# Issuing a third of the expert weights' transfers from the Activation queue in a two-layer MoE encoder

## The chip, the cores and the metric

The kernel runs on one core of a Trainium2 chip. The metric is the device time of one execution in microseconds (us). The engines are named PE (TensorE, matmuls), PEld (its weight loads), DVE (VectorE), ACT (ScalarE), POOL (GpSimd) and SP (SyncE, which here issues transfers and computes nothing). A name with a q (SPq) means the engine's instruction queue: what it issues or waits for itself. Transfers are done by 16 DMA engines that all issuing engines share.

## The reference, cut to what matters

An encoder trunk of two layers over 256 tokens of 1024 numbers, all float32. Layer 0 mixes tokens with causal pooling, layer 1 with differential attention. Each layer then has a mixture of experts: 32 experts, each token goes to two of them.

```python
for i in range(DEPTH):                       # 2 layers
    h = rms_norm(x, norm_mix_g[i])
    x = x + (pool_mixer(...) if i % 2 == 0 else diff_attention(...))
    h = rms_norm(x, norm_ffn_g[i])
    x = x + hier_moe(h, ...)
return rms_norm(x, final_g)

# in hier_moe, for the tokens xb of each expert e:
a = jax.nn.silu(xb @ w1[e]) * (xb @ w3[e])   # w1, w3: 1024 x 512
y = a @ w2[e]                                # w2: 512 x 1024
```

Each of w1, w3 and w2 has 2 MB per expert, so the experts' weights are 6 MB each and 403 million bytes in all; each weight is used once.

## The kernel before

**Order.** The five engines each run an instruction stream written out by hand, and wait for each other by semaphores. The pooling mixer, the router, the experts of layer 0, attention, the router and the experts of layer 1 follow each other. The router's numbers (`cnt`, a place for each token) are ready before the expert loop starts (`s_route`).

**The ring.** Expert weights come into `ring`, eight slots (`RING = 8`) of 2 MB each. An expert takes three chunks (`CPE = 3`): chunk 0 has the first half of w1 and of w3 (along the contracted dimension), chunk 1 the second half of both, chunk 2 all of w2. Each chunk is two transfers of 1 MB, which add to one semaphore, `loaded[slot]`. Chunk number c of a layer (c = 3e + j for chunk j of expert e) lies in slot c % 8. All 192 chunks of the two layers, and attention's eight chunks between them, are issued by SP, in exactly this order of numbers. SP issues the first eight of layer 0 at the start; those of layer 1 as attention's own chunks are used up (`attn_used`). Every later chunk c waits (L279) until chunk c - 8 is used: that is the semaphore `half` where c - 8 is a chunk 0 (PE has done the products with the first half), `gu` where it is a chunk 1 (the gate and up products are done), `y` where it is a chunk 2 (the down product is done). So w2 of expert e + 2 follows `half` of expert e; the first half of w1 and w3 of expert e + 3 follows `gu` of expert e; their second half follows `y` of expert e. In layer 0, attention's chunks follow behind the last expert's on the same queue.

**The expert loop.** Each of PE, DVE, ACT and SP runs four iterations (`ITERS = 4`) of eight experts (`BODY = 8`), in groups of four experts (`E4 = 4`). For one expert PE does the gate and up products (`gate_up`, L427, two halves of 32 matmuls; up to 32 tokens; a second block if there are more), gathers tokens of the next group (`gather`, L394), waits for the activated product, transposes it (L447), and does the down product (`down`, L465). After four experts the results are added to the tokens (`scatter`, L480). Between `gu` and the transpose stand: on ACT the Exp (L730), then on DVE one plus, reciprocal and two products (L1022 to L1028). ACT then copies the gathered tokens (L720), at the second expert of a group also the gates (L734), and after the down product its half of the result (L738); DVE copies the transposed product (L1051) and the other half (L1054). `keep_clock` issues matmuls whose results nobody reads (L346).

**The stages around it.** After the last expert of a layer follow the scatter, the residual sum on DVE (L1088), the norm, and in layer 0 the transposes (L338) and attention's products (L586 for v, L600 for q and k, L654 for the output); in layer 1 the final norm and the store of the result. POOL loads two rows of gains during attention (L327, L329), repeated over 128 partitions.

**The fallback.** If an expert had more than 64 tokens, more passes would follow, for which SP loads all chunks again (L291 to L301). In this case's data it does not run.

Of the kernel before, what the change touches and what calls it, by code (L numbers as in the profile page):

```python
# [35 lines left out]
E4 = P // SB  # L36
GPB = 2
BODY = GPB * E4
ITERS = NE // BODY
# [54 lines left out]
def build(nc, x, norm_mix_g, norm_ffn_g, pool_w, pool_scale, wq, wk, wv, wo, lq1, lk1, lq2, lk2, subln_g,  # L94
          moe_wg, moe_bg, moe_we, moe_be, moe_w1, moe_w3, moe_w2, final_g, consts, out):
    with ExitStack() as ctx:
# [122 lines left out]
        def chunk_parts(layer, e, j):  # L219

            if j < 2:
                return [(m * 2048, w[layer, e, :, :].rearrange("(p k) n -> p k n", k=KT)[:, 4 * j:4 * j + 4, :])
                        for m, w in ((0, moe_w1), (1, moe_w3))]
            w = moe_w2[layer, e, :, :].rearrange("(j p) n -> p j n", p=P)
            return [(m * 2048, w[:, 2 * m:2 * m + 2, :]) for m in range(2)]
# [17 lines left out]
        def _(sp):  # L243
# [25 lines left out]
            for layer in range(2):  # L269
                for c in range(RING):  # L270
                    if layer == 1:
                        sp.wait_ge(*attn_used[c])
                    load(c, chunk_parts(layer, c // CPE, c % CPE), loaded[c])
                steady = CPE * BODY

                def stream(it, c):

                    e, j = divmod(c - RING, CPE)
                    sp.wait_ge(used[j], it * BODY + (layer * NE + e + 1))  # L279
                    load(c % RING, chunk_parts(layer, it * BODY + c // CPE, c % CPE), loaded[c % RING])  # L280

                with sp.Fori(0, ITERS - 1) as it:
                    for c in range(RING, RING + steady):
                        stream(it, c)
                for c in range(RING, steady):
                    stream(ITERS - 1, c)

                fb = more[layer]
                sp.wait_ge(s_route, layer + 1)
                most = sp.value_load(cnt[0:1, NE + NGRP:NE + NGRP + 1], min_val=0, max_val=S)  # L290
                with sp.If(most > CAP):  # L291

                    sp.wait_ge(main["y"], NE * (layer + 1))
                    with sp.Fori(0, PASSES - 1) as m:
                        with sp.If(most > CAP * m + CAP):
                            with sp.Fori(0, NE) as e:
                                n = m * NE + e
                                for j in range(CPE):
                                    load(j, chunk_parts(layer, e, j), fb[f"wl{j}"])
                                sp.wait_ge(fb["y"], n + 1)  # L300
                                sp.sem_inc(fb["passed"], 1)  # L301
                if layer == 0:
                    for c in range(ACH):
                        e, j = divmod(CPE * NE - RING + c, CPE)
                        sp.wait_ge(used[j], e + 1)
                        load(c, attn_parts(c), loaded[c])
# [386 lines left out]
        def _(act_e):  # L693
# [29 lines left out]
                for r in range(E4):  # L723
                    gathered(s, 0, r, rounds + r + 1)

            def group(s, g, u, rounds):
                for k in range(E4):
                    n1 = g * E4 + (k + 1)
                    act_e.wait_ge(s["gu"], n1)
                    act_e.activation(sg[:, 0, :, :], gu_ps[:, :, 0, :], ACT.Exp, scale=-1.0).then_inc(s["exp"], 1)  # L730
                    gathered(s, 1 - u, k, rounds + k + 1)
                    if k == 1:
                        act_e.wait_ge(s["gt"], g + 1)
                        act_e.copy(gateT[:, :, :], gt_ps).then_inc(s["gtc"], 1)  # L734

                    act_e.wait_ge(s["y"], n1)
                    for i in (2, 3):
                        ins = act_e.copy(y[SB * k:SB * (k + 1), :, 256 * i:256 * (i + 1)],  # L738
                                         y_ps[SB * i:SB * (i + 1), :, :])
                    ins.then_inc(s["yc_a"], 1)  # L740

            def experts(layer):
                act_e.wait_ge(s_route, layer + 1)
                first_gathered(main, layer * (NGRP + 1) * E4)
                with act_e.Fori(0, ITERS) as it:
                    for gg in range(GPB):
                        group(main, it * GPB + (layer * NGRP + gg), gg % 2,
                              it * (GPB * E4) + (layer * (NGRP + 1) + gg + 1) * E4)
                fb = more[layer]
                most = act_e.value_load(cnt[0:1, NE + NGRP:NE + NGRP + 1], min_val=0, max_val=S)  # L750
                with act_e.If(most > CAP):
                    with act_e.Fori(0, PASSES - 1) as m:
                        with act_e.If(most > CAP * m + CAP):
                            first_gathered(fb, m * ((NGRP + 1) * E4))
                            with act_e.Fori(0, NGRP // 2) as pair:
                                for u in range(2):
                                    group(fb, m * NGRP + pair * 2 + u, u, (m * (NGRP + 1) + pair * 2 + (u + 1)) * E4)

            def route(layer):

# [458 lines left out]
```

## Time and profile before

| | us |
|---|---|
| median of three runs | 1174.48 |
| lowest and highest | 1172.45, 1177.19 |
| the profiled execution | 1172.21 |
| its span (first to last instruction) | 1170.4 |
| PE busy | 888.4 |
| DVE busy | 352.2 |
| ACT busy | 216.5 |
| transfers | 427.70 MB, 365 GB/s over the span |

The profile is of one execution. Each time in it is from the start of its span. A row of a view names the line of the kernel, the engine, the operation, and what it writes and reads; `x` is a count. An idle time in brackets stands before the instruction that ended it, with what released it; "issue" is idle time that no semaphore explains. The row of an issued transfer is the time that the issuing engine spends on it; the landing is reported separately. The clock named PEclk is the share of full speed that PE was granted.

### The profile page before, as it was taken

The numbers are of one execution on the slowest core, as the hardware profiler recorded it, in microseconds if no ns is written. First come the engines' busy times: TensorE is split into PE (matmuls) and PEld (weight loads), VectorE is DVE, ScalarE is ACT, GpSimd is POOL, SyncE is SP. The second block draws the span as 40 slices with busy tenths as digits, with TensorE's granted clock in tenths as the row PEclk, the third lists the DMA queues.
The fourth block names the chain that finished last, engine by engine and source line by source line (L and its number), as shares of the span: only waits on it lengthen the run. The fifth ranks groups of instructions, "written<-read, shape, count | busy, mean of one in ns | idle before, by whom it ended". The sixth has DMA issues, their size and how long they took to land.

```text
span 1170.4 us, 20054 instructions
## 1 busy us (share of the span) xinstructions
PE 888.4 (76%) x8020; PEld 496.3 (42%) x8021; DVE 352.2 (30%) x814; ACT 216.5 (18%) x487; POOL 5.1 (0%) x15
## 2 busy tenths in 40 slices
PE   6878777766776677678999987898776757677765
PEld 4544434332433343333787554454433423334332
DVE  3523322221331222223156433222322312222223
ACT  3221212110111111111145312111111111112111
POOL 1000000000000000000000000000000000000000
PEclk9899979988998889899999989999998999888898
DMA  9979999999999999998503439999999999999992
GB/s 307 399 311 414 415 415 416 416 416 415 416 416 416 415 415 416 416 416 353 199 1 147 173 141 418 415 416 416 415 415 415 415 416 416 417 414 416 416 413 114
DMA packets 78121, 427.70 MB, mean 365 GB/s; under 512 B 7492, under 2 KB 8772, under 8 KB 43672
## 3 DMA queue, kind: packets, MB, share of 16 engines
q1 hardware_dynamic: 77528, 424.20, 88.8%
q8 instruction: 131, 2.15, 0.7%
q0 software_dynamic: 448, 1.25, 0.5%
q14 instruction: 14, 0.11, 0.0%
HBM read 424.37 MB, written 1.05 MB: 363 GB/s over the span
## 4 chain that ended last, share of the span: by engine, by line
SPq 41%; PE 30%; DMA 19%; DVE 5%; issue 4%; ACT 2%; DVEq 0%; ACTq 0%
SPq L247 40%; DMA ring<-in_moe_w 18%; PE ps L427 7%; PE ps L600 5%; PE ps L465 3%; PE ps L586 2%; PE ps L394 2%; PE ps L480 2%; PE ps L654 2%; DVE work L1024 1%; PE ps L379 1%; PE ps L346 1%; PE ps L561 1%; PE ps L374 1%; PE ps L338 1%
## 5 line engine op out<-in xcount | busy, mean ns | idle before, releaser
L427 PE MATMUL ps<-ring,work 128*32 128x256 f32 x4224 | 304.6, 437 | 178.7 <-DMA ring<-in_moe_w 123.9
L427 PEld LDWEIGHTS ps<-ring,work 128*32 128x32 f32 x4224 | 144.3, 123 | 331.3 <-DMA ring<-in_moe_w 151.2
L394 PE MATMUL ps<-work,h_sb 128*128 128x256 f32 x576 | 153.5, 412 | 7.1 <-ACT work L720 4.5
L1022 DVE TENSOR_SCALAR work<-work 128x128 f32<-128x128 f32 (+1 forms) x64 | 14.7, 230 | 476.5 <-ACT work L730 476.5
L465 PE MATMUL ps<-ring,work 128*32 128x256 f32 x2112 | 129.3, 386 | 25.7 <-DVE work L1051 25.5
L394 PEld LDWEIGHTS ps<-work,h_sb 128*128 128x128 f32 x576 | 110.2, 202 | 59.0 <-issue 38.6
L1054 DVE COPY hT<-ps 32x512 f32<-32x512 f32 x128 | 87.4, 683 | 139.5 <-PE ps L465 138.6
L730 ACT ACTIVATE work<-ps 128x256 f32<-128x256 f32 x64 | 24.6, 384 | 485.3 <-PE ps L427 485.3
L738 ACT COPY hT<-ps 32x512 f32<-32x512 f32 x128 | 74.1, 579 | 169.0 <-PE ps L465 168.3
L465 PEld LDWEIGHTS ps<-ring,work 128*32 128x32 f32 x2112 | 63.4, 110 | 75.6 <-DVE work L1051 32.7
L480 PE MATMUL ps<-hT,work 128*128 128x512 f32 x136 | 62.6, 604 | 11.1 <-DVE hT L1054 11.1
L720 ACT COPY work<-ps 128x512 f32<-128x512 f32 x72 | 42.2, 586 | 132.1 <-PE ps L394 126.7
L1024 DVE RECIPROCAL work<-work 128x128 f32<-128x128 f32 (+1 forms) x64 | 62.6, 978 | 2.2
L600 PE MATMUL ps<-hT,ring 128*128 128x256 f32 x256 | 56.5, 379 | 0.0
L600 PEld LDWEIGHTS ps<-hT,ring 128*128 128x128 f32 x256 | 48.2, 190 | 7.1 <-issue 0.5
L346 PE MATMUL ps<-cst,small 128*128 128x512 f32 x78 | 43.5, 645 | 3.5 <-issue 3.5
L480 PEld LDWEIGHTS ps<-hT,work 128*128 128x128 f32 x136 | 24.5, 189 | 49.2 <-issue 49.2
L447 PE MATMUL ps<-cst,work 128*128 128x128 f32 x64 | 20.7, 323 | 29.1 <-DVE work L1028 28.7
L1051 DVE COPY work<-ps 128x256 f32<-128x256 f32 x64 | 27.2, 425 | 50.0 <-PE ps L447 50.0
L447 PEld LDWEIGHTS ps<-cst,work 128*128 128x128 f32 x64 | 9.1, 142 | 56.7 <-issue 56.6
L654 PE MATMUL ps<-ring,work 128*128 128x512 f32 x64 | 28.6, 594 | 0.0
L586 PE MATMUL ps<-ring,hT 128*128 128x512 f32 x64 | 27.9, 594 | 0.8 <-DVE hT L918 0.8
(151 smaller groups left out, 454.9 us busy)
## 6 DMA issues: line engine op xcount, KB each, us to landing
ring<-in_moe_w SPq DMA_DIRECT2D x384, 1024.0 KB, 21.8
ring<-in_attn_wv SPq DMA_DIRECT2D x4, 1024.0 KB, 18.5
ring<-in_attn_wq SPq DMA_DIRECT2D x4, 1024.0 KB, 20.3
ring<-in_attn_wk SPq DMA_DIRECT2D x4, 1024.0 KB, 22.7
ring<-in_attn_wo SPq DMA_DIRECT2D x4, 1024.0 KB, 21.5
x_sb<-in_x SPq DMA_DIRECT2D x2, 512.0 KB, 6.3
work<-in_pool_w SPq DMA_DIRECT2D x1, 1024.0 KB, 12.9
out_x<-h_sb SPq DMA_DIRECT2D x2, 512.0 KB, 2.7
```

Of the source, the lines that this page charges most:

```text
L247: sp.dma_start(ring[:, slot, at:at + k * n].rearrange("p (k n) -> p k n", k=k), src) \
L346: pe.matmul(ps[:, bank, :], zero, cst[:, 0:512], start=True, stop=True)
L394: mm = pe.matmul(xg_ps[:, q, :], h_sb[:, t, kt * P:(kt + 1) * P], onehot[:, u, t].rearrange("p b e s -> p (b e s)"), start=(t == 0), stop= ...
L427: mm = pe.matmul(gu_ps[SB * j:SB * (j + 1), b, :, :], xg[:, u, 4 * half + q, b, k, :], w[:, :, q, P * j:P * (j + 1)], start=(half == 0 and ...
L465: mm = pe.matmul(y_ps[SB * i:SB * (i + 1), b, :], actT[:, b, SB * j:SB * (j + 1)], w[:, j, 256 * i:256 * (i + 1)], start=(j == 0 and b == ...
L480: mm = pe.matmul(acc[:, t, i, :], gateT[:, b, t * P:(t + 1) * P], y[:, b, 512 * i:512 * (i + 1)], start=False, stop=False, skip_group_chec ...
L586: mm = pe.matmul(ps[:, 2 * t + i, :], hT[:, kt, t * P:(t + 1) * P], matrix(0, kt)[:, 512 * i:512 * (i + 1)], start=(kt == 0), stop=(kt == ...
L600: mm = pe.matmul(ps[:, h % 2, i * S:(i + 1) * S], matrix(2 + 2 * i, kt)[:, h * P:(h + 1) * P], hT[:, kt, :], start=(kt == 0), stop=(kt == ...
L654: mm = pe.matmul(ps[:, 2 * t + i, :], qT[:, h, t * P:(t + 1) * P], matrix(6, h)[:, 512 * i:512 * (i + 1)], start=(h == 0), stop=(h == NH - 1))
L738: ins = act_e.copy(y[SB * k:SB * (k + 1), :, 256 * i:256 * (i + 1)], y_ps[SB * i:SB * (i + 1), :, :])
L1024: ve.reciprocal(sg[:, 2, b, :], sg[:, 1, b, :]).then_inc(s["sig"], 1)
L1054: ins = ve.tensor_copy(y[SB * k:SB * (k + 1), :, 256 * i:256 * (i + 1)], y_ps[SB * i:SB * (i + 1), :, :])
```

## The change

The transfers of chunk 2 (w2) of experts 2 to 31 of each layer leave SP's stream and are issued by ACT, into ACT's own hardware queue. SP issues in the loop only chunks 0 and 1, under the same waits as before. ACT issues w2 of expert e + 2 in expert e, directly behind its wait for `gu` of expert e and ahead of the Exp. Since `gu` comes after `half` of the same expert, no wait of its own is added for the slot. The first eight chunks of a layer, which include w2 of experts 0 and 1, are still SP's, as are attention's chunks and the fallback. So that nothing is issued beyond expert 31, ACT's loop runs three iterations, and the fourth is written out behind it.

```diff
                 with sp.Fori(0, ITERS - 1) as it:
                     for c in range(RING, RING + steady):
-                        stream(it, c)
+                        if c % CPE < 2:
+                            stream(it, c)
                 for c in range(RING, steady):
-                    stream(ITERS - 1, c)
+                    if c % CPE < 2:
+                        stream(ITERS - 1, c)
...
-            def group(s, g, u, rounds):
+            def down_weights(layer, it, k):
+
+                c = CPE * (k + 2) + 2
+                for at, src in chunk_parts(layer, it * BODY + (k + 2), 2):
+                    n, m = view(src)
+                    act_e.dma_start(ring[:, c % RING, at:at + n * m].rearrange("p (k n) -> p k n", k=n), src) \
+                        .then_inc(loaded[c % RING], 16)
+
+            def group(s, g, u, rounds, load):
                 for k in range(E4):
                     n1 = g * E4 + (k + 1)
                     act_e.wait_ge(s["gu"], n1)
+                    load(k)
                     act_e.activation(sg[:, 0, :, :], gu_ps[:, :, 0, :], ACT.Exp, scale=-1.0).then_inc(s["exp"], 1)
...
-                with act_e.Fori(0, ITERS) as it:
+                def body(it, last):
                     for gg in range(GPB):
+                        def load(k, gg=gg):
+                            if not last or gg * E4 + k + 2 < BODY:
+                                down_weights(layer, it, gg * E4 + k)
+
                         group(main, it * GPB + (layer * NGRP + gg), gg % 2,
-                              it * (GPB * E4) + (layer * (NGRP + 1) + gg + 1) * E4)
+                              it * (GPB * E4) + (layer * (NGRP + 1) + gg + 1) * E4, load)
+
+                with act_e.Fori(0, ITERS - 1) as it:
+                    body(it, False)
+                body(ITERS - 1, True)
```

## Rows read from the trace of the kernel before

**Rows 1.** The page: span, and GB/s of all transfers in 40 equal slices.
```profile
span 1170.4 us, 20054 instructions
...
GB/s 307 399 311 414 415 415 416 416 416 415 416 416 416 415 415 416 416 416 353 199 1 147 173 141 418 415 416 416 415 415 415 415 416 416 417 414 416 416 413 114
```

**Rows 2.** Stretches (us): each engine's busy time, PEclk, DMA share, GB/s.
```profile
200.00:280.00 80.00, 57.30 (x581) 29.24 (x582) 21.97 (x45) 12.37 (x23) 0.00 (x0) 0.91 1.02 416
...
570.00:578.00 8.00, 8.00 (x38) 7.03 (x38) 0.00 (x0) 0.65 (x2) 0.00 (x0) 1.00 1.01 405
...
1143.00:1156.00 13.00, 8.10 (x78) 4.16 (x72) 2.18 (x5) 0.97 (x2) 0.00 (x0) 0.87 0.34 139
```

**Rows 3.** Groups by line: count, busy us, mean ns, idle us before with its releasers.
```profile
L427 PE MATMUL ps<-ring,work 128*32 128x256 f32 x4224 | 304.6, 437 | 178.7 <-DMA ring<-in_moe_w 123.9 <-issue 53.3 <-ACT work L720 1.5
...
L427 PEld LDWEIGHTS ps<-ring,work 128*32 128x32 f32 x4224 | 144.3, 123 | 331.3 <-DMA ring<-in_moe_w 151.2 <-issue 121.4
...
L465 PEld LDWEIGHTS ps<-ring,work 128*32 128x32 f32 x2112 | 63.4, 110 | 75.6 <-DVE work L1051 32.7 <-issue 7.7 <-DMA ring<-in_moe_w 1.7
```

**Rows 4.** The page: the chain that ended last, by engine, share of span.
```profile
SPq 41%; PE 30%; DMA 19%; DVE 5%; issue 4%; ACT 2%; DVEq 0%; ACTq 0%
```

**Rows 5.** L247 from 200 to 480 us: issue in ns (min/median/max), landing after it.
```profile
L247 SPq DMA_DIRECT2D ring<-in_moe_w x110: 383/2144/5955, 198.4 to 478.4; - x110
...
DMA to landing us min/median/max: 14.6/22.1/24.7
```

**Rows 6.** SP in order of time at both restarts: start, us, instructions merged.
```profile
64.31 0.99 SPq L247 DMA_DIRECT2D ring<-in_moe_w  x2
...
66.03 0.34 SPq L247 DMA_DIRECT2D ring<-in_moe_w  x1
...
698.47 0.97 SPq L247 DMA_DIRECT2D ring<-in_moe_w  x2
...
700.67 0.35 SPq L247 DMA_DIRECT2D ring<-in_moe_w  x1
...
706.07 0.81 SPq L247 DMA_DIRECT2D ring<-in_moe_w  x2
```

**Rows 7.** The last w2 issue of each layer (line L247): start, landing after it.
```profile
L247 SPq DMA_DIRECT2D ring<-in_moe_w x1: 2292/2292/2292, 497.0 to 497.0; - x1
...
DMA to landing us min/median/max: 22.7/22.7/22.7
...
L247 SPq DMA_DIRECT2D ring<-in_moe_w x1: 2287/2287/2287, 1129.8 to 1129.8; - x1
...
DMA to landing us min/median/max: 23.8/23.8/23.8
```

**Rows 8.** PE in order of time behind the last chunks of both layers.
```profile
514.60 1.93 PE L427 MATMUL ps<-ring,work 128*32 128x256 f32 x32 [3.09 <-DMA ring<-in_moe_w]
...
536.83 10.57 PE L586 MATMUL ps<-ring,hT 128*128 128x512 f32 x24 [0.78 <-DVE hT L918]
...
1148.68 3.35 PE L427 MATMUL ps<-ring,work 128*32 128x256 f32 x32 [4.38 <-DMA ring<-in_moe_w]
...
1155.54 1.93 PE L465 MATMUL ps<-ring,work 128*32 128x256 f32 x32 [0.52 <-DVE work L1051]
```

**Rows 9.** ACT's Exp in order of time: experts 0, 8, 16; 0, 2, 29.
```profile
65.88 0.38 ACT L730 ACTIVATE work<-ps 128x256 f32<-128x256 f32 x1 [3.87 <-PE ps L427]
...
172.23 0.38 ACT L730 ACTIVATE work<-ps 128x256 f32<-128x256 f32 x1 [17.22 <-PE ps L427]
...
295.13 0.38 ACT L730 ACTIVATE work<-ps 128x256 f32<-128x256 f32 x1 [17.06 <-PE ps L427]
...
700.51 0.38 ACT L730 ACTIVATE work<-ps 128x256 f32<-128x256 f32 x1 [4.36 <-PE ps L427]
...
720.08 0.39 ACT L730 ACTIVATE work<-ps 128x256 f32<-128x256 f32 x1 [4.03 <-PE ps L427]
...
1120.89 0.38 ACT L730 ACTIVATE work<-ps 128x256 f32<-128x256 f32 x1 [9.00 <-PE ps L427]
```

More of the change, by code:

```diff
@@ L756, in experts @@
                                 for u in range(2):
-                                    group(fb, m * NGRP + pair * 2 + u, u, (m * (NGRP + 1) + pair * 2 + (u + 1)) * E4)
+                                    group(fb, m * NGRP + pair * 2 + u, u, (m * (NGRP + 1) + pair * 2 + (u + 1)) * E4, lambda k: None)
             def route(layer):
```

## The prediction, made before the change was built

> **What bounds the kernel now.** Read the slices first: outside the start, the attention stage and the end, the transfers run at 413 to 418 GB/s [rows 1]. In a stretch of the loop the DMA share is 1.02 and the rate 416 [rows 2]. TensorE's largest wait there is for the ring at L427, the gate and up products: 123.9 us, and 151.2 us on its weight loads; at L465, the down product, the weight loads wait 1.7 us for a DMA [rows 3]. So w2 is there in time already; what comes too late is w1 and w3, and above all the second half of them. I name the chunks of expert k a(k), b(k) (its two halves of w1 and w3) and w2(k), k from 0 to 31 in a layer; each is two transfers of 1 MB.
>
> The chain puts 41% on SP's queue, L247 [rows 4], and in the loop a transfer's issue takes SP 2.14 us in the median and up to 5.96 [rows 5]. That looks like an issue bound and isn't one: with few transfers outstanding a pair of issues takes 0.97 to 0.99 us and the first alone 0.34 or 0.35 of a next pair [rows 6], so the rest of the 2.14 us is SP held back by a full queue. Transfers land 14.6 to 24.7 us after issue in the loop [rows 5]; at 2.5 us for 1 MB (416 GB/s) that is up to some nine outstanding. The kernel is bound by the rate of the transfers, and SP's queue is served in the order in which TensorE needs the chunks.
>
> From this follows a layer's length. The transfers stop once the ring's 8 chunks are full and start again when the first chunk is freed: at 64.31 and 698.47 us [rows 6]. From there they never stop until w2(31) has landed: issued at 497.0, landed 22.7 later, 519.7; and 1129.8 + 23.8 = 1153.6 [rows 7]. That is 455.4 and 455.1 us. The last chunk that TensorE waits for is b(31): its products start at 514.60 and 1148.68, after waits of 3.09 and 4.38 us for the DMA, while the last down product starts at 1155.54 behind DVE, not behind w2 [rows 8]. b(31) lands one chunk, 5 us, ahead of w2(31), and all that follows hangs on it.
>
> **The change part by part.**
>
> *Moved issues.* 30 chunks a layer, w2(2) to w2(31): 120 of the 384 transfers go from SP to ACT; the first 8 chunks of a layer stay with SP, as does the fallback. Bytes and slots are the same, so at the same rate a layer's stretch from restart to last landing stays 455.4 and 455.1 us. SP gives up issues that were waits for room: nothing gained.
>
> *The wait.* w2(k+2) took the slot of a(k) and was issued after a(k)'s products (`half`); now ACT issues it after b(k)'s (`gu`). In the loop that is no delay: SP issued the second half of the last w2 at 1129.8, and ACT sees the `gu` of two experts back at 1120.89, 9 us before [rows 7, 9]. At the restart it is one: there `half` of expert 0 starts the engines, and the next chunk, a(3), comes with `gu` at 66.03 and 700.67, so **+1.7 and +2.2 us** [rows 6]. They don't run dry again behind it: two chunks start together, 10 us of work, and b(3) was issued 5.4 us after a(3) (706.07 in layer 1, [rows 6]).
>
> *The order at the end.* With two queues w2(31) no longer stands behind b(31). When TensorE has done b(29), ACT issues w2(31); still to come are a(30), b(30), a(31), b(31) and w2(31), 25 us. If the engines share half and half, w2(31) is through after 10 us, at one third after 15, both before b(31) at 25. So b(31) lands last, where w2(31) did: at 66.03 + 455.4 = 521.4 against 514.6 (**+6.8**, of which 5.1 is the order and 1.7 the restart). The chain behind it up to the attention matmuls is TensorE, DVE and ACT, and attention's own chunks aren't in it: v's products start at 536.83 behind DVE [rows 8], while their two chunks follow w2(31) at 5 us each, some 530. Layer 1 restarts at 700.67 + 6.8 = 707.5; plus 455.1 is 1162.6 against 1148.68, **+13.9 us** in all. What follows b(31) to the end, 21.7 us, stays.
>
> *ACT's time.* Each expert gets two issues ahead of the Exp. Between 0.97 us for a pair (SP with an empty queue, [rows 6]) and 4.3 (twice its median in the loop, [rows 5]), longer if held as SP was at worst. Behind the Exp are four DVE steps, the transpose and the down product; behind it on ACT also the gather's copy, which TensorE's next gather needs. I take 1.0, since ACT's own queue holds two to four transfers, not nine. What hides it: experts 0 to 7 of layer 0, which mostly find their chunks loaded, take 172.23 - 65.88 = 106.4 us, the next eight 122.9, so TensorE has 16.5 us over in eight experts, 2.1 each [rows 9]. At 4.3 that cover is gone; the rival below prices it. The last two experts issue nothing.
>
> *Loop peeled on ACT, more code in it.* TensorE's own loop turns stand in these times, and no slice of the loops falls under 413 GB/s for them [rows 1]; a turn on ACT lies under the same cover. Zero; up to 1 us a turn is hidden too.
>
> *Two queues on the same engines.* The nearest row is the stretch in which POOL's loads of gains (L327, L329) run beside SP's: share 1.01, 405 GB/s, against 1.02 and 416 for one queue [rows 2]. So from nothing to 2.7% of 910 us, +24.6 us. POOL's loads repeat one row 128 times, which ACT's don't, so I take zero.
>
> The Trainium skill ("DMA: Bandwidth & Descriptors", section "Queues, rings and completion order") says that each DMA engine goes round robin over the queues with work, packet by packet; by it w2(31) passes b(31) as assumed, and no run before this one shows it. If instead the order of issue held, the sum would be 1178.4.
>
> **Sum.** 1.7 + 5.1 + 2.2 + 4.9 = 13.9. The profiled execution took 1172.2 us with a span of 1170.4; the median of three is 1174.5; the span stands in [rows 1]. Span 1184.3, median 1174.5 + 13.9 = **1188.4 us**, +1.2%.
>
> **The rivals.**
> - *ACT is held at its issues* (slower still). If SP's blocked issue keeps ACT waiting, a pair costs 4.3 us or more ahead of the Exp, over the 2.1 of cover. For it: SP is in L247 nearly without a break in the loop. Against: it corrects itself, since a later TensorE frees slots later, SP's queue empties and issues are short again; the engines stay busy. It costs where no backlog is left, at the end: from b(29)'s products to b(31)'s there are 25 us, and two experts take 19.6 at TensorE's best (700.51 to 720.08, [rows 9]), so 5.4 are over; of a delay of 4.3 on each of the two issues before them, and of products at the lower clock (3.35 us for a half instead of 1.93, [rows 8]), about 4 a layer comes out: 1196.5. A chance of 0.12. The Trainium skill ("Perfetto Trace Analysis", section "DMA Instruction — HWDGE (DVE, Sync)") says that the descriptor generator is locked by one sequencer until its descriptors are made; it would be the mechanism of this rival.
> - *Two queues cost rate*: 405 instead of 416 gives 1188.4 + 24.6 = 1213. It decides from 0.3% of rate, 3 us. A chance of 0.10.
> - *w2 stays last* (no change). If ACT's queue is served behind SP's backlog, b(31) lands as before and only the restarts remain: 1174.5 + 3.9 = 1178.4, within 0.5%. For it: SP's backlog is large. Against: w2 would then have to get less than a fifth of the engines over 25 us, and the down products, starved all along, would show it. Here too belongs a partial gain at the ragged end: from 1143 to 1156 us the share is 0.34, some DMA engines being done long before the last [rows 2]; if two queues took half of that out, 4 to 5 us a layer, the sum is about 1179. A chance of 0.15 for both.
> - *SP's issuing is the bound* (faster). For it: 41% of the chain. A third of its issues gone, up to 120 x 2.14 = 257 us; TensorE's waits at L427 cap it at 123.9, so down to 1050, and any tenth of that, 12 us, makes it 1162 with nothing lost. The Trainium skill ("Perfetto Trace Analysis", section "DMA Optimizations") advises to spread transfers over issuing engines where the issuing engine's track is solid; here it is. Against: issues of 0.35 us on an empty queue, and a rate that never leaves 416. With other gains of rate from two queues 0.11.
> - *The code doesn't do what it says*: 120 issues would be missing on ACT's queue; the diff leaves no way for that. 0.01, at the old time.
>
> **How the numbers follow.** The forecast has 0.51, with its own range of 1184 to 1194 (TensorE at the lower clock behind b(31), 1.5 us a layer, and up to 2 us a layer if its last two experts don't keep up). Over the rivals the range is 1175 to 1213: it leaves out the faster case and what lies above 1213, under 2 in 10. A run of this kernel can tell about 0.5%, 5.9 us. Slower by more: 0.51 + 0.12 + 0.10 = 0.73; within: 0.16; faster: 0.11.
>
> **What would show it.** Right: 120 L247-like issues on ACT's queue, a pair near 1 us; SP's median issue well under 2 us; the engines' restart at `gu`; the last landing being w1 or w3 of expert 31, TensorE's longest wait before b(31), then 21 to 22 us to the end; rate 414 to 417 still. TensorE's waits at L427 grow by some 5 us a layer plus what now isn't waited elsewhere. Wrong: a rate under 412 or above 420 in the loops; Exp starting over 2 us behind `gu` as a rule; the down products waiting for the ring; w2(31) landing after b(31).

## The result, and the profile after

The changed kernel takes 1189.72 us (median of four runs, 1188.56 to 1191.48) beside 1174.57 us for the kernel before, executed alongside it: a ratio of 1.0129, with a 95% interval of 1.0104 to 1.0155, or 15.2 us. Forecast were 13.9 us. The profiled execution took 1188.56 us with a span of 1186.8, which is 16.4 more than [rows 1].

First the page of the kernel after: span, slices of GB/s, the chain by engine, and the transfers of each issuing engine (count, KB each, median us to landing).

```profile
span 1186.8 us, 20061 instructions
...
GB/s 308 389 293 415 415 414 416 415 416 415 415 416 415 416 416 414 416 418 297 177 1 141 176 113 408 415 415 416 413 415 415 416 414 416 416 416 415 416 393 86
...
PE 50%; DMA 25%; DVE 10%; issue 7%; ACTq 4%; ACT 2%; DVEq 0%; SPq 0%
...
ring<-in_moe_w SPq DMA_DIRECT2D x264, 1024.0 KB, 24.0
ring<-in_moe_w ACTq DMA_DIRECT2D x120, 1024.0 KB, 22.6
```

Set beside [rows 1, 4]: 120 transfers have moved, the loops still run at 413 to 418 GB/s (408 in the slice that holds the restart of layer 1), and SP's 41% of the chain has become nothing. A third of the issues went to another engine, the engine that stood for 41% of the chain isn't on it any more, and the kernel is slower. The two loops as one stretch each (columns as in [rows 2]) say the same, 416 and 415 against 416:

```profile
200.00:280.00 80.00, 56.15 (x618) 30.19 (x611) 20.73 (x42) 12.65 (x24) 0.00 (x0) 0.91 1.02 416
...
750.00:1100.00 350.00, 258.12 (x2776) 137.49 (x2776) 94.16 (x188) 53.39 (x100) 0.00 (x0) 0.93 1.02 415
```

So nothing is lost in the loops. What is lost lies at their two ends. The timeline of the kernel after has both ends of both layers: start and duration in us, what, and in brackets the idle time before it.

```profile
66.40 0.83 SPq L247 DMA_DIRECT2D ring<-in_moe_w  x2
66.40 1.03 ACTq L734 DMA_DIRECT2D ring<-in_moe_w  x2
67.47 0.38 ACT L742 ACTIVATE work<-ps 128x256 f32<-128x256 f32 x1 [5.09 <-issue]
...
517.77 1.91 PE L430 MATMUL ps<-ring,work 128*32 128x256 f32 x32
522.61 1.93 PE L430 MATMUL ps<-ring,work 128*32 128x256 f32 x32 [2.93 <-DMA ring<-in_moe_w]
...
538.93 5.49 PE L349 MATMUL ps<-cst,small 128*128 128x512 f32 x6 [3.51 <-issue]
...
710.72 1.00 ACTq L734 DMA_DIRECT2D ring<-in_moe_w  x2
...
1164.91 2.94 PE L430 MATMUL ps<-ring,work 128*32 128x256 f32 x32 [3.25 <-DMA ring<-in_moe_w]
...
1171.89 1.93 PE L468 MATMUL ps<-ring,work 128*32 128x256 f32 x32 [0.52 <-DVE work L1071]
```

At 66.40 us SP issues a(3) and ACT issues w2(2) in the same moment; in [rows 6] the engines were started 1.7 us ahead of that by `half`. And where b(31)'s products started at 514.60 and 1148.68 us [rows 8], they start at 522.61 and 1164.91.

The last issues of each queue in layer 1 (issue in ns, time of issue, and then us to landing), first SP's b(31), then ACT's second half of w2(31):

```profile
L247 SPq DMA_DIRECT2D ring<-in_moe_w x1: 433/433/433, 1131.6 to 1131.6; - x1
...
DMA to landing us min/median/max: 33.2/33.2/33.2
...
L734 ACTq DMA_DIRECT2D ring<-in_moe_w x1: 488/488/488, 1140.2 to 1140.2; - x1
...
DMA to landing us min/median/max: 22.3/22.3/22.3
```

b(31) is issued 8.6 us ahead of w2(31) and lands 2.3 us behind it: 1131.6 + 33.2 = 1164.8 against 1140.2 + 22.3 = 1162.5. TensorE starts on it 0.1 us later. In [rows 7] it was w2(31) that landed last, at 1153.6, 4.9 us behind the start of b(31)'s products. In layer 0 it is the same: b(31) at 522.6 (490.2 + 32.4), w2(31) at 519.7 (494.4 + 25.3).

The lead of w2(31) is small because it isn't alone in ACT's queue: w2(30), whose second half was issued at 1125.4 us, lands only at 1147.6, 7.8 us after w2(31) was issued, and w2(31) follows 14.9 us behind it. Its row:

```profile
L734 ACTq DMA_DIRECT2D ring<-in_moe_w x1: 378/378/378, 1125.4 to 1125.4; - x1
...
DMA to landing us min/median/max: 22.2/22.2/22.2
```

**Where the 16.4 us of the span are**, each stretch before and after:

| stretch | before | after | more |
|---|---|---|---|
| start to first restart | 64.31 | 66.40 | 2.1 |
| restart to b(31)'s products, layer 0 | 450.3 | 456.2 | 5.9 |
| from there to SP's first expert chunk of layer 1 (before 565.47, after 574.80) | 50.9 | 52.2 | 1.3 |
| from there to the second restart (698.47, 710.72) | 133.0 | 135.9 | 2.9 |
| restart to b(31)'s products, layer 1 | 450.2 | 454.2 | 4.0 |
| from there to the end | 21.7 | 21.9 | 0.2 |

Of the 2.1, 1.7 are the step from `half` to `gu`; the other 0.4 had come up before it. Of the 2.9, 2.2 are that step. The stretch from restart to last landing was 455.4 and 455.1 us before; after, it is 456.2 and 454.1.

The groups of TensorE in the loop and of the instruction that waits for it, after (L430, L468, L450 are the L427, L465, L447 of before):

```profile
L430 PE MATMUL ps<-ring,work 128*32 128x256 f32 x4224 | 280.1, 410 | 113.3 <-DMA ring<-in_moe_w 63.0 <-issue 48.6 <-ACT work L723 1.5
...
L468 PE MATMUL ps<-ring,work 128*32 128x256 f32 x2112 | 164.2, 465 | 28.9 <-DVE work L1071 24.4 <-DMA ring<-in_moe_w 4.1
...
L450 PE MATMUL ps<-cst,work 128*128 128x128 f32 x64 | 21.2, 332 | 101.3 <-DVE work L1048 100.8 <-issue 0.4
```

And two of these groups in the kernel before:

```profile
L465 PE MATMUL ps<-ring,work 128*32 128x256 f32 x2112 | 129.3, 386 | 25.7 <-DVE work L1051 25.5
...
L447 PE MATMUL ps<-cst,work 128*128 128x128 f32 x64 | 20.7, 323 | 29.1 <-DVE work L1028 28.7 <-issue 0.2
```

TensorE waits 60.9 us less for the ring at the gate and up products (123.9 in [rows 3], now 63.0) and 72.1 us more at the transpose (28.7, now 100.8), behind ACT's issues: 1.2 us for each of the 60 experts that issue. This looks like a 72 us loss and a 61 us gain. It is neither, it is the same slack in another place; a4_behind_exp, below, moves it back. Along with the idle time went the lower clock: the down products behind it take 34.9 us more busy time (129.3, now 164.2) and the gate and up products 24.5 less (304.6, now 280.1).

### The profile page after: what moved, and what is told of

Same layout as the page of the kernel before. It is cut to its first block, busy times and chain, and to the rows that moved or that the text cites. A ratio compares the mean times of both kernels' runs of the same rounds, so it can differ in the third digit from the quotient of the medians.

```text
span 1186.8 us, 20061 instructions
## 1 busy us (share of the span) xinstructions
PE 895.0 (75%) x8020; PEld 503.4 (42%) x8021; DVE 352.0 (30%) x814; ACT 215.7 (18%) x487; POOL 5.1 (0%) x15
## 4 chain that ended last, share of the span: by engine, by line
PE 50%; DMA 25%; DVE 10%; issue 7%; ACTq 4%; ACT 2%; DVEq 0%; SPq 0%
DMA ring<-in_moe_w 24%; PE ps L430 15%; PE ps L468 10%; PE ps L483 5%; PE ps L603 5%; ACTq L734 4%; DVE work L1044 3%; PE ps L397 2%; PE ps L589 2%; PE ps L657 2%; DVE work L1071 1%; PE ps L349 1%; ACT work L742 1%; PE ps L450 1%; DVE work L1048 1%
## 5 line engine op out<-in xcount | busy, mean ns | idle before, releaser
L430 PE MATMUL ps<-ring,work 128*32 128x256 f32 x4224 | 280.1, 410 | 113.3 <-DMA ring<-in_moe_w 63.0
L430 PEld LDWEIGHTS ps<-ring,work 128*32 128x32 f32 x4224 | 142.4, 118 | 248.4 <-issue 105.0
L468 PE MATMUL ps<-ring,work 128*32 128x256 f32 x2112 | 164.2, 465 | 28.9 <-DVE work L1071 24.4
L397 PE MATMUL ps<-work,h_sb 128*128 128x256 f32 x576 | 149.0, 402 | 6.4 <-ACT work L723 4.5
L397 PEld LDWEIGHTS ps<-work,h_sb 128*128 128x128 f32 x576 | 107.1, 196 | 53.7 <-issue 34.6
L468 PEld LDWEIGHTS ps<-ring,work 128*32 128x32 f32 x2112 | 73.8, 129 | 95.0 <-issue 40.9
L450 PE MATMUL ps<-cst,work 128*128 128x128 f32 x64 | 21.2, 332 | 101.3 <-DVE work L1048 100.8
L450 PEld LDWEIGHTS ps<-cst,work 128*128 128x128 f32 x64 | 9.0, 140 | 131.7 <-issue 131.7
## 6 DMA issues: line engine op xcount, KB each, us to landing
ring<-in_moe_w ACTq DMA_DIRECT2D x120, 1024.0 KB, 22.6
```

What stands on the lines that cost most here:

```text
L397: mm = pe.matmul(xg_ps[:, q, :], h_sb[:, t, kt * P:(kt + 1) * P], onehot[:, u, t].rearrange("p b e s -> p (b e s)"), start=(t == 0), stop= ...
L430: mm = pe.matmul(gu_ps[SB * j:SB * (j + 1), b, :, :], xg[:, u, 4 * half + q, b, k, :], w[:, :, q, P * j:P * (j + 1)], start=(half == 0 and ...
L468: mm = pe.matmul(y_ps[SB * i:SB * (i + 1), b, :], actT[:, b, SB * j:SB * (j + 1)], w[:, j, 256 * i:256 * (i + 1)], start=(j == 0 and b == ...
```

## The experiments

My theory, from the prediction: the kernel is bound by the rate of the transfers, and the loss is made of two things that have nothing to do with who issues. The order of the last two landings is swapped (b(31) last instead of w2(31)), and the engines restart at `gu` instead of `half`. Its rivals: what is lost comes from ACT's time at its issues, or from two queues sharing the engines.

**Each part alone, on SP's one queue.** These three start from the kernel before, and ACT issues nothing in them. b1_order swaps the last two chunks of each layer:

```diff
-                for c in range(RING, steady):
+                for c in (*range(RING, steady - 2), steady - 1, steady - 2):
                     stream(ITERS - 1, c)
```

> The kernel before with one queue as it was; only the last two chunks of each layer change places in SP's stream, so that w2 of expert 31 goes ahead of the second half of w1 and w3 of expert 31. My theory (the order of the last landings is worth 5.1 and 4.9 us, and no second queue is needed for it): +10.0 us over the kernel before, 1184.5. Rival 'two queues or ACT's hold make the loss': 1174.5, since neither is in this kernel.

Measured: 1186.53 us beside 1173.08, a ratio of 1.0119 (1.0099 to 1.0140): 13.5 us by the medians, 14.0 by the ratio; 10.0 had been expected, and the interval (11.6 to 16.4 us) leaves that out. TensorE's timeline at both ends of b1_order:

```profile
520.34 3.64 PE L427 MATMUL ps<-ring,work 128*32 128x256 f32 x32 [8.20 <-DMA ring<-in_moe_w]
...
528.15 1.93 PE L465 MATMUL ps<-ring,work 128*32 128x256 f32 x32 [0.52 <-DVE work L1051]
...
1162.07 3.64 PE L427 MATMUL ps<-ring,work 128*32 128x256 f32 x32 [9.17 <-DMA ring<-in_moe_w]
...
1169.87 1.93 PE L465 MATMUL ps<-ring,work 128*32 128x256 f32 x32 [0.52 <-DVE work L1051]
```

and the clock over the first of these groups of products (columns as in [rows 2]):

```profile
520.30:524.00 3.70, 3.67 (x33) 1.48 (x33) 0.00 (x0) 0.00 (x0) 0.00 (x0) 0.50 1.01 423
```

Behind 8.2 us of idle time TensorE has a granted clock of 0.50, its 1.2 GHz level, and the 32 matmuls take 3.64 us instead of 1.93; behind the 9.17 of layer 1 they take 3.64 too. From the start of b(31)'s products to the down product there are 7.81 and 7.80 us; in the kernel before 5.43 and 6.86 (514.60 to 520.03, and 1148.68 to 1155.54 [rows 8]). That is 2.4 + 0.9 = 3.3 us on top of the 10.0 of the order: 13.3. In the trace the order itself is 5.1 and 4.9 us, as forecast: from the restarts (64.90 and 706.92) to b(31)'s products there are 455.4 and 455.2 us, against 450.3 and 450.2.

In layer 0 of the changed kernel this doesn't occur, although b(31) lands just as late. There the transfers of w2 share the engines with those ahead of b(31) and hold them back: a(31) lands at 516.5 us (issued at 481.15, landed 35.3 later), its products start at 517.77, and b(31)'s wait is only 2.93 us. Over b(31)'s products the clock is 1.00:

```profile
522.60:524.50 1.90, 1.89 (x33) 0.97 (x33) 0.00 (x0) 0.00 (x0) 0.00 (x0) 1.00 1.00 414
```

In layer 1 b(31)'s products take 2.94 us behind 3.25 of waiting, at a clock of 0.64; from their start to the down product there are 6.98 us, nearly the 6.86 of the kernel before. A short wait alone doesn't settle the clock: behind 3.0 to 3.1 us the same 32 matmuls took 1.93 us in layer 0 of the kernel before and of b2_wait_gu, but 3.44 in a1_half and 3.53 and 3.62 in b4_hold5.

b2_wait_gu lets SP wait for `gu` where it waited for `half`:

```diff
-                    sp.wait_ge(used[j], it * BODY + (layer * NE + e + 1))
+                    sp.wait_ge(used[max(j, 1)], it * BODY + (layer * NE + e + 1))
```

> The kernel before with one queue in the same order; only w2 of experts 2 to 31 waits for the gate and up products of two experts back (gu) instead of the first half of them (half). My theory: only the restart of the transfers in each layer moves, +1.7 and +2.2, so +3.9 us, 1178.4. Rival 'a later wait costs all along the loop': up to 1.9 us for each of 60 experts, over 1200. Rival 'the restart is hidden': 1174.5.

Measured: 1177.49 us beside 1173.08, 1.0035 (1.0021 to 1.0049), 4.1 to 4.4 us: as expected. Its SP queue at the restarts, to be set against [rows 6]:

```profile
66.84 0.99 SPq L247 DMA_DIRECT2D ring<-in_moe_w  x2
...
705.36 0.97 SPq L247 DMA_DIRECT2D ring<-in_moe_w  x2
```

The first restart is 2.5 us later than there (1.7 for the step to `gu`, and 0.8 that stand ahead of it), the second 6.9 us in all.

b3_order_wait has both edits.

> Both of the last two in one kernel, still with one queue and nothing on ACT. My theory: they add up to the whole loss less what the second queue and ACT's issues cost: 1174.5 + 13.9 = 1188.4 against 1189.7 for the changed kernel. Rival 'the second queue or ACT's hold makes a large part': clearly under 1185.

Measured: 1189.47 us beside 1173.08, 1.0137 (1.0113 to 1.0161), 16.1 to 16.4 us. The interval holds the changed kernel's 1.0129. A kernel with one queue, nothing issued by ACT and nothing new in its instruction stream is as slow as the changed one, once it has its order and its wait. As to size, the 3.3 us of clock are in this run and not in the changed kernel, so the two agree less closely than their times make it seem (b(31)'s products take 3.47 and 3.64 us in it, behind 8.18 and 7.97 us of waiting).

**The changed kernel with its parts undone.** a1_half gives ACT the earlier wait:

```diff
+                    act_e.wait_ge(s["half"], n1)
+                    load(k)
                     act_e.wait_ge(s["gu"], n1)
-                    load(k)
```

> The changed kernel, but ACT waits for half of the expert, issues w2 of two experts on, and then waits for gu; w2 of expert 31 stays in ACT's queue. My theory: the restart term goes (3.9 us), the order term stays: 11 us over the kernel before (ratio 1.0095). Rival 'ACT's issues ahead of the Exp make the loss': they no longer hold the Exp here, so the loss falls by more than the restart, to under 8 us.

Measured: 1185.86 us beside 1174.61, 1.0092 (1.0072 to 1.0111), 10.8 us, which fits the 11 of the theory and not the rival's under 8.

a2_last_sp leaves w2(31) with SP, in its old place behind b(31):

```diff
-                    if c % CPE < 2:
+                    if c % CPE < 2 or c == steady - 1:
...
-                            if not last or gg * E4 + k + 2 < BODY:
+                            if not last or gg * E4 + k + 2 < BODY - 1:
```

> The changed kernel, only w2 of expert 31 of each layer is issued by SP again, behind the second half of w1 and w3 of expert 31; all else on ACT as changed, behind gu and ahead of the Exp. My theory: the order term goes, 10 us by the landings and 13.5 by what the order alone had cost with one queue; left are the restart's 3.9 and 1 to 2 for the second queue and ACT's issues: 4 to 6 us over the kernel before (ratio 1.0035 to 1.005). Rival 'the loss lies in the loop': over 10.

Measured: 1179.20 us beside 1174.61, 1.0043 (1.0026 to 1.0059), 5.0 us, inside the 4 to 6 expected.

a3_half_last has both edits. 116 transfers are still issued by ACT.

> The changed kernel with two edits: ACT waits for half of the expert, issues w2 of two experts on, and only then waits for gu; and w2 of expert 31 is SP's again, behind the second half of w1 and w3 of expert 31. 58 of the 60 w2 chunks stay in ACT's queue. My theory: both terms are gone, 1174.5 to 1177 (what is left is the cost of the second queue and of ACT's issues). Rival 'two queues cost rate or ACT's issues cost time': it stays above 1183.

Measured: 1175.79 us beside 1173.08, 1.0022 (1.0009 to 1.0036), 2.6 us. What is left of the loss when order and restart are mended is these 2.6 us (1.1 to 4.2): the second queue, ACT's issues, and a longer code together. It isn't zero, and the runs don't divide it. Undoing the wait gives 4.4 us back (15.2 to 10.8) and undoing the order 10.2 (15.2 to 5.0). For the wait that is the size of doing it alone (4.1 to 4.4); for the order it is the 10.0 of the landings and not the 14.0 that it cost alone, since the changed kernel had not paid b1_order's 3.3 us of clock.

**ACT's time, and what covers it.** a4_behind_exp issues w2 behind the Exp instead of ahead of it, with the same waits and the same order:

```diff
-                    load(k)
                     act_e.activation(sg[:, 0, :, :], gu_ps[:, :, 0, :], ACT.Exp, scale=-1.0).then_inc(s["exp"], 1)
+                    load(k)
```

> The changed kernel with ACT's two issues moved from ahead of the Exp to right behind it. My theory: the hold of 1.0 us an expert lies under TensorE's waits for the ring, so nothing but 0.5 us of later restart in each layer: as the changed kernel, ratio to the kernel before 1.012 to 1.014. Rival 'the hold costs time': 1 us less for each expert that isn't covered, so a ratio under 1.010.

Measured: 1188.80 us beside 1174.61, 1.0121 (1.0096 to 1.0147), 14.2 us, so nothing to be told from the changed kernel. Its groups, as above:

```profile
L430 PE MATMUL ps<-ring,work 128*32 128x256 f32 x4224 | 299.5, 431 | 177.5 <-DMA ring<-in_moe_w 119.3 <-issue 56.7 <-ACT work L723 1.5
...
L450 PE MATMUL ps<-cst,work 128*128 128x128 f32 x64 | 20.4, 318 | 29.5 <-DVE work L1048 29.2 <-issue 0.2
```

The wait at the transpose falls from 100.8 to 29.2 us, the wait for the ring grows from 63.0 to 119.3 at the gate and up products and from 4.1 to 21.5 at the down products, and the time stays. That is what "covered" means: the 72.1 us behind ACT's issues had cost nothing that shows beside intervals of some 3 us either way.

To measure the cover without a second queue, b4_hold5 and b5_hold12 put 5 and 12 small copies ahead of the Exp in the kernel before:

```diff
+                    for q in range(5):
+                        act_e.copy(work2[:, 2048 + 16 * q:2064 + 16 * q], cst[:, 0:16])
                     act_e.activation(sg[:, 0, :, :], gu_ps[:, :, 0, :], ACT.Exp, scale=-1.0).then_inc(s["exp"], 1)
```

> The kernel before; ACT does five copies of 16 columns of a constant into scratch ahead of each Exp, some 1 us, as long as the changed kernel's two issues hold it. My theory (TensorE has 2.1 us an expert over): no change in time (ratio 0.998 to 1.002); TensorE's waits for DVE ahead of the transpose grow by some 60 us and those for the ring fall by as much. Rival 'a hold ahead of the Exp is on the path': 60 us more.

> The same with twelve copies, some 2.4 us an expert or more. It asks where the cover ends. My theory: it is 2.1 us in the mean over eight experts, so 0.3 us or more an expert comes out, some 20 us in all if the copies take 2.4 us, and each further 0.1 us adds 6; a quarter of the experts finds less cover than the mean, the ring's backlog evens that out. If the cover were only that of the worst expert, 100 us more; if there is more cover than I read, nothing.

The holds came out shorter than I had wanted, since copies overlap: each takes 200 ns, but all of them together 40.1 us for 64 experts, 0.63 us each, and with 12 copies 87.5 us, 1.37 us each. The group of the copies and the transpose in b4_hold5:

```profile
L731 ACT COPY work<-cst 128x16 f32<-128x16 f32 x320 | 40.1, 200 | 441.5 <-PE ps L427 441.5
...
L447 PE MATMUL ps<-cst,work 128*128 128x128 f32 x64 | 20.8, 326 | 64.6 <-DVE work L1030 64.3 <-issue 0.2
```

and in b5_hold12:

```profile
L731 ACT COPY work<-cst 128x16 f32<-128x16 f32 x768 | 87.5, 200 | 365.1 <-PE ps L427 365.1
...
L427 PE MATMUL ps<-ring,work 128*32 128x256 f32 x4224 | 278.9, 409 | 89.0 <-issue 49.5 <-DMA ring<-in_moe_w 37.6 <-ACT work L720 1.5
...
L447 PE MATMUL ps<-cst,work 128*128 128x128 f32 x64 | 21.4, 334 | 113.9 <-DVE work L1030 113.9
```

Measured: 1176.38 and 1176.69 us beside 1174.63, 1.0011 (0.9997 to 1.0025) and 1.0017 (1.0004 to 1.0029). 87.5 us of work on the path from `gu` to the transpose cost 2.0 us; the wait for the ring gives the rest, 37.6 us of it being left. Where the cover ends on one queue these runs don't show, since the longest hold came to 1.37 us an expert.

a5_hold5 puts the 5 copies into the changed kernel, ahead of the Exp and behind the two issues.

> The changed kernel with five such copies ahead of each Exp, behind its two issues: some 2.1 us of hold in all, the whole cover as I read it. My theory: 0 to 6 us over the changed kernel, ratio to the kernel before 1.012 to 1.019. If the changed kernel has used its cover up already: 60 us more, ratio near 1.06.

Measured: 1195.53 us beside 1174.63, 1.0176 (1.0148 to 1.0203), 20.7 us by the ratio, 5.5 more than the changed kernel's 15.2. The two intervals still touch (1.0148 and 1.0155), but the trace shows that here the cover ends. Its slices of GB/s, its wait for the ring, and the loop of layer 1:

```profile
GB/s 308 385 302 415 416 415 396 416 416 414 416 416 415 416 414 415 416 417 267 176 1 191 178 118 411 416 416 390 351 415 414 415 415 416 415 415 415 416 396 72
```

```profile
L430 PE MATMUL ps<-ring,work 128*32 128x256 f32 x4224 | 278.9, 410 | 73.2 <-issue 52.2 <-DMA ring<-in_moe_w 19.3 <-ACT work L723 1.5
```

```profile
750.00:1100.00 350.00, 264.94 (x2748) 140.52 (x2737) 92.35 (x185) 64.94 (x217) 0.00 (x0) 0.90 1.00 408
```

With 1.0 + 0.63 us ahead of each Exp only 19.3 us of waiting for the ring are left, and three slices fall to 396, 390 and 351 GB/s: TensorE frees slots too late there for the transfers to go on. In layer 1 this is behind an expert with a second block of tokens and the scatter: nothing is issued between 826.4 and 839.1 us, the last transfer under way lands at 837.0, and from 835 to 840 us the rate is 28 GB/s. At 408 instead of 415 GB/s, 350 us of layer 1 lose 350 x 7 / 415 = 5.9 us. The changed kernel stands some 0.6 us per expert away from this.

**The order in layer 1 alone.** b6_order_layer1 has b1_order's swap in the second layer only, to divide its 14 us.

```diff
-                for c in range(RING, steady):
+                for c in (*range(RING, steady - 2), *((steady - 2, steady - 1), (steady - 1, steady - 2))[layer]):
```

> The kernel before with one queue; the last two chunks change places in layer 1 only. Both layers together had cost 13.5 us where the landings give 10.0. If the excess comes from the stretch between the layers (TensorE at a lower clock behind a later last chunk), this kernel costs 4.9 us, 1.0042; if it comes from each layer's end alike, 6.7 us, 1.0057.

Measured: 1179.29 us beside 1174.63, 1.0054 (1.0033 to 1.0074): 4.7 us by the medians, 6.3 by the ratio, with an interval of 3.9 to 8.7 that holds both expectations. The profile says more: b(31)'s products again have 3.64 us and 8.52 us of idle time before them. Of the 5.3 us that its span is longer, 4.2 come up to them and 1.1 behind, so a part of the excess belongs to the layer's own end.

```profile
1152.88 3.64 PE L427 MATMUL ps<-ring,work 128*32 128x256 f32 x32 [8.52 <-DMA ring<-in_moe_w]
```

**How the engines share two queues.** A pair of w2 transfers, 2 MB, takes 5 us at 416 GB/s if it has the engines to itself, 10 at a half of them and 15 at a third. At the restart of layer 0 ACT's pair is issued together with SP's pair for a(3). The second of ACT's two in the kernel after, issued at 67.0 us:

```profile
L734 ACTq DMA_DIRECT2D ring<-in_moe_w x1: 396/396/396, 67.0 to 67.0; - x1
...
DMA to landing us min/median/max: 18.8/18.8/18.8
```

It lands 19.4 us after the restart at 66.40 (67.0 + 18.8 - 66.4). w2's transfers have runs of 4 KB, those of w1 and w3 runs of 8 KB. a7_wide_rows gives w2's the same 8 KB, by reading it with its rows in another order; its result is not the reference's, and it was executed once:

```diff
-                for at, src in chunk_parts(layer, it * BODY + (k + 2), 2):
+                w = moe_w2[layer, it * BODY + (k + 2), :, :].rearrange("(m p q) n -> m p q n", m=2, q=2)
+                for at, src in ((m * 2048, w[m]) for m in range(2)):
```

> The changed kernel, but ACT's transfers read w2 so that each partition's run is 8 KB long instead of two of 4 KB; the rows of w2 then land in another order in the ring, so the output is not the reference's; work and bytes are the same. It asks how the engines share the two queues. If they take one run from each queue in turn, ACT's share was a third (4 KB against 8 KB) and becomes a half: the pair of w2 transfers issued at the restart lands within some 15 us instead of 19.5, the first of the two after 9 instead of 12. If they share by bytes or by transfers, nothing changes there. In either case the second half of expert 31's w1 and w3 is the last to land, and the time stays within 3 us of the changed kernel.

ACT's transfers in a7_wide_rows, over the whole run, and then the second one at the restart (the restart is at 66.30 us here):

```profile
L735 ACTq DMA_DIRECT2D ring<-in_moe_w x120: 335/369/1290, 66.3 to 1142.3; - x120
...
DMA to landing us min/median/max: 8.0/12.2/15.4
...
L735 ACTq DMA_DIRECT2D ring<-in_moe_w x1: 360/360/360, 66.9 to 66.9; - x1
...
DMA to landing us min/median/max: 13.5/13.5/13.5
```

The pair has landed 14.1 us after the restart at the latest (66.9 + 13.5 - 66.3) instead of 19.4, which is about the 5 us between a half and a third; over the run a w2 transfer lands in 12.2 us in the median instead of 22.6. One landing doesn't settle it, though: at the restart of layer 1 the same pair lands 14.5 us behind the restart in the changed kernel and 14.3 in a7_wide_rows, because in the changed kernel SP's next pair starts only when its first is nearly through, and ACT's runs get 0.83 of the bytes from 720.7 to 722.7 us.

The records of the single runs in the trace do settle it. Where both queues have work, from 1140 to 1150 us in the changed kernel, 331 runs of 8 KB and 349 of 4 KB start, which gives w2 0.35 of the bytes; in a7_wide_rows, from 69 to 76 us, 179 and 179 of 8 KB, which gives it 0.50. On an engine the next run's record starts 3 to 4 ns before the end of the one ahead of it (in the kernel before 627 of the 653 runs from 300 to 310 us have such a successor), so the order can be followed: in that stretch of a7_wide_rows 399 pairs of records stand so, and every one is of two different queues; in the changed kernel's 630 of 681 are, and about 40 of the other 51 are what chance would pair. So each engine takes one run from each queue in turn, not a group of them. The time, 1186.2 us in one execution, says only that the kernel stays slow: b(31) is still last.

## Why the prediction was right, step by step

- **The bound.** Right. The rate stays at 415 to 416 GB/s with a third of SP's issues gone. SP's issues became short, 382 ns in the median over the run instead of 2144 in [rows 5], and the time that they had taken turned into SP waiting for slots. The issues of both engines after:

```profile
L247 SPq DMA_DIRECT2D ring<-in_moe_w x264: 327/382/6828, 14.0 to 1131.6; - x132
...
L734 ACTq DMA_DIRECT2D ring<-in_moe_w x120: 375/442/1545, 66.4 to 1140.2; - x120
```

  These are SP's waits after (us in total, times, longest):

```profile
SPq L247 <- PE ps L430: 399.5, 60, 30.1
SPq L247 <- PE ps L468: 378.3, 60, 10.1
```

  and before:

```profile
SPq L247 <- PE ps L427: 127.8, 36, 27.2
...
SPq L247 <- PE ps L465: 45.6, 13, 5.2
```

- **The wait, +1.7 and +2.2.** Right, and measured by itself: 4.1 to 4.4 us for 3.9 (b2_wait_gu), 4.4 given back (a1_half).
- **The order at the end, +5.1 and +4.9.** Right in the mechanism: b(31) last. In size, the trace of after has 5.9 and 4.0 from restart to b(31)'s products, together 9.9 for 10.0. Of the two cases that I gave for the sharing, a half and a third, it was the third. But w2(31) was to be through 15 us after its issue at a third, 10 us ahead of b(31); it took 22.7 (1139.8 to 1162.5) and was ahead by 2.3 us, and by 2.9 in layer 0. My list of what was still to come left out w2(30), which stood before it in ACT's queue for another 7.8 us. The price of the order is the same for any lead, so the sum didn't suffer. But the margin against the rival *w2 stays last* was much thinner than the prediction has it.
- **The stretch from restart to last landing stays.** Within 1 us: 456.2 and 454.1 for 455.4 and 455.1. It held within 1.2 us in all kernels but two, a5_hold5 (461.2 in layer 1) and a7_wide_rows (451.6 and 457.6).
- **ACT's two issues take 1.0 us and are hidden.** Right: 1.03 and 1.00 us at the restarts, 0.442 us for one in the median over the run, 1.545 at most. Hidden, as a4_behind_exp shows. The cover itself was taken too large: 2.1 us an expert was a mean over eight, and at a hold of 1.6 us (a5_hold5) the rate already falls. I had read a mean where the stretch with the least cover decides, here an expert with two blocks.
- **Loop peel and second queue, zero.** Not quite: a3_half_last leaves 2.6 us (1.1 to 4.2) for these and ACT's issues. The stretch that I took as bound, 405 GB/s beside POOL's loads, wasn't near.
- **What follows b(31) stays.** 21.9 for 21.7 us in layer 1. In layer 0 not quite: 1.3 us are lost between b(31) and q and k, and 0.7 beyond the `gu` step before the second restart. The fillers there take 5.49 us where they took 4.25, at a lower clock. b2_wait_gu has the same 5.49 without a change of order:

```profile
533.34 5.49 PE L346 MATMUL ps<-cst,small 128*128 128x512 f32 x6 [3.25 <-issue]
```

  so it isn't the order. What decides how long they get the lower clock stays open.
- **What would show it.** One sign was named wrongly: TensorE's waits at the gate and up products should have grown and fell by 60.9 us, because ACT's issues, which I had called hidden, took their place. A hidden cost still shows in the waits, it only doesn't show in the time. A sign that was to mean *wrong* came up as well, the down products waiting for the ring: two of them, 4.1 us in all, and 21.5 in a4_behind_exp at the same time of the kernel. It was no sign of anything that costs.

The terms sum to 13.9, the timed runs give 15.2 (12.2 to 18.2). In the profile's 16.4 the surplus is 0.4 before the first restart and some 2 us in and ahead of attention.

**The rivals.** *ACT is held at its issues* fell: 1.545 us at worst, while SP's were up to 6.8. The generator's lock which the Trainium skill describes ("Perfetto Trace Analysis", section "DMA Instruction — HWDGE (DVE, Sync)") can't be seen as a cost here; what had held SP was its own queue, and ACT's has about three transfers outstanding (two for every 15 us of an expert, each landing after 22.6: an estimate). *Two queues cost rate* fell: 416 and 415. *w2 stays last* fell: it passes b(31) by 2.3 and 2.9 us. The rule by which it does ("DMA: Bandwidth & Descriptors", section "Queues, rings and completion order", in the Trainium skill) is borne out in that the queues are served in turn. The page's turn is a packet of several descriptors; in the records above it is one run, and the measurement decides. *SP's issuing is the bound* fell most plainly: SP is at 0% of the chain and the kernel is 1.3% slower. The Trainium skill ("Perfetto Trace Analysis", section "DMA Optimizations") says that balancing transfers over issuing engines may help if the issuing engine looks busy with slices, as opposed to actual DMA time. SP looked busy and was held back, while the DMA engines were at their rate, so this was not the page's case (the prediction's sentence on the page leaves its condition out); the length of an issue on an empty queue, 0.34 us in [rows 6] against 2.14 in [rows 5], tells the two apart.

No kernel of the study is faster than the one before. The nearest with ACT's queue is a3_half_last, at 1.0022.

## What to carry to other kernels

Here the DMA engines were at their rate all through the loops, and moving issues to another engine bought nothing; only two moments counted, when the engines start again and which chunk lands last. A second queue breaks the order of one: what is issued later on it can pass what TensorE needs first (w2(31), issued 8.6 us behind b(31), landed 2.3 us ahead of it), so keep the last chunks on one queue in the order of use. Ahead of such a change, compare the issue of a transfer on an empty queue with its median in the loop: if the second is much longer and the rate of the transfers stays level, as here (0.34 and 2.14 us, 416 GB/s), the issuing engine is being held and isn't the bound.

## What the runs showed of the hardware

- Two hardware queues shared the DMA engines one run at a time, whatever the size of the run: where both had work, ACT's 4 KB runs beside SP's 8 KB runs got 0.35 of the bytes (changed kernel, 1140 to 1150 us), its 8 KB runs 0.50 (a7_wide_rows, 69 to 76 us), and there each of 399 pairs of runs that follow each other was of two queues.
- An issue took 2.14 us in the median with one queue, 0.38 and 0.44 with two, for the same transfers at the same rate. The number of transfers in the queue doesn't explain it alone: with eight outstanding on SP's queue an issue took 2.10 us in the median before, a third of them with 4 KB runs, and 0.38 after, all with 8 KB runs (190 to 290 us). What the limit counts stays open.
- Behind 8.0 to 9.2 us of waiting, 32 matmuls of TensorE took 3.47 to 3.64 us instead of 1.93 (five cases in b1_order, b3_order_wait and b6_order_layer1), in the first of them at a granted clock of 0.50 (the 1.2 GHz level). Behind 2.9 to 3.3 us they took anything from 1.93 to 3.62: 1.93 in layer 0 of the changed kernel, 2.94 in its layer 1, 3.62 in b4_hold5.
- Small copies on ACT overlap: five of 200 ns took 0.63 us, twelve 1.37.
